# Wide blocks of a hybrid decoder trunk: all 512-column products of a block ahead of all its 256-column products

## The reference, cut to what matters

```python
    for i in range(DEPTH):
        h = rms_norm(x, norm1_g[i]) * (1.0 + sc1) + sh1
        if i % N_MIXERS == 0:
            mix = dilated_attention(h, attn_w_in[j], attn_w_out[j])
        else:
            mix = s5_mixer(h, ssm_w_in[j], ...)
        x = x + g1 * mix
        h = rms_norm(x, norm2_g[i]) * (1.0 + sc2) + sh2
        x = x + g2 * conv_ffn(h, ffn_w_up[i], ffn_conv_w[i], ffn_conv_b[i], ffn_w_down[i])
```

## Time and profile before

| | before |
|---|---|
| median of 3 runs | 2727.33 us (2723.91 to 2728.22) |
| span of the profiled execution | 2724.8 us |
| TensorE busy, matmuls | 2659.1 us (98%), 18416 |
| TensorE busy, weight loads | 2376.3 us (87%) |
| VectorE busy | 2299.6 us (84%) |
| ScalarE busy | 1294.9 us (48%) |
| GpSimd busy | 518.8 us (19%) |
| mean granted TensorE clock | 0.990 |

### The profile page before, as it was taken

The page is one execution under the profiler, slowest core; times in us unless marked ns, Lnnn a source line. Parts: engine busy times, 40 slices in busy tenths (PEclk is TensorE's granted clock), DMA queues, the critical chain, the costliest instruction groups (busy, mean ns, idle before and its releaser), DMA issues.

```text
span 2724.8 us, 50038 instructions
## 1 busy us (share of the span) xinstructions
PE 2659.1 (98%) x18416; PEld 2376.3 (87%) x18416; DVE 2299.6 (84%) x3379; ACT 1294.9 (48%) x1869; POOL 518.8 (19%) x468
## 2 busy tenths in 40 slices
PE   6999999999999999999999999999999999999998
PEld 2998888888898888888889998999888888888887
DVE  6978988888889998899999988998898975677754
ACT  2444444444434555435555344444365553455543
POOL 4242211101132111000111321244411110011122
PEclk8999999999999999999999999999999999999999
DMA  9989989889876987678888967779777766655563
GB/s 388 386 268 342 344 313 338 314 314 334 317 225 226 320 283 245 203 253 311 283 279 275 375 221 230 235 249 332 254 256 252 257 182 190 194 190 187 182 189 116
DMA packets 242267, 725.47 MB, mean 266 GB/s; under 512 B 51106, under 2 KB 60066, under 8 KB 241186
## 3 DMA queue, kind: packets, MB, share of 16 engines
q1 hardware_dynamic: 185184, 666.46, 71.1%
q10 hardware_dynamic: 56900, 56.54, 6.6%
HBM read 701.66 MB, written 25.44 MB: 267 GB/s over the span
## 4 chain that ended last, share of the span: by engine, by line
PE 84%; DVE 4%; POOL 1%; DMA 1%; issue 1%; ACT 1%; ACTq 0%; DVEq 0%; POOLq 0%
PE proj L1936 40%; PE proj L1939 22%; PE proj L1959 5%; PE proj L1960 5%; PE proj L1961 5%; PE proj L1941 3%; PE proj L1954 1%; DVE w_lo L1201 1%; PE proj L1957 1%; PE ps L2077 1%; PE ps L2167 1%; ACT w_hi L605 0%; DVE work L1484 0%; PE pturn L2194 0%; POOL work L1784 0%
## 5 line engine op out<-in xcount | busy, mean ns | idle before, releaser
L605 ACT ACTIVATE w_hi<-raw 128x1024 fp32r<-128x1024 f32 (+1 forms) x896 | 933.0, 1044 | 992.1 <-PE proj L1939 355.2
L1201 DVE TENSOR_TENSOR w_lo<-raw,w_hi 128x1024 fp32r<-128x1024 f32 (+1 forms) x896 | 1107.2, 1238 | 288.7 <-ACT w_hi L605 276.7
L1936 PE MATMUL proj<-h_hl,w_hi 128*128 128x512 f32 x3990 | 1007.5, 393 | 2.6 <-DVE x L1531 1.7
L1936 PEld LDWEIGHTS proj<-h_hl,w_hi 128*128 128x128 f32 x3990 | 730.5, 189 | 139.2 <-DVE x L1531 2.1
L1939 PEld LDWEIGHTS proj<-h_hl,w_lo 128*128 128x128 f32 x4256 | 580.6, 190 | 41.5
L1939 PE MATMUL proj<-h_hl,w_lo 128*128 128x256 f32 x4256 | 593.4, 282 | 0.0
L1091 DVE SCALAR_TENSOR_TENSOR ada<-ada,held 128x1024 f32<-128x1024 f32 x304 | 392.4, 1291 | 0.0
L1834 POOL TENSOR_TENSOR a_hl<-work,a_hl 128x256 fp32r<-128x256 f32 (+1 forms) x88 | 119.7, 1360 | 1137.3 <-ACT a_hl L895 1137.3
L1959 PE MATMUL proj<-a_hl,w_hi 128*128 128x256 f32 x864 | 245.6, 284 | 0.7 <-DVE a_hl L1422 0.6
L1960 PE MATMUL proj<-a_hl,w_hi 128*128 128x256 f32 x864 | 244.6, 283 | 0.0
L1961 PE MATMUL proj<-a_hl,w_lo 128*128 128x256 f32 x864 | 244.5, 283 | 0.0
(11 more groups left out here) (279 smaller groups left out, 2873.3 us busy)
## 6 DMA issues: line engine op xcount, KB each, us to landing
raw<-in_w_up SPq DMA_DIRECT2D x352, 512.0 KB, 4.9
ada<-in_ada_t SPq DMA_DIRECT2D x304, 512.0 KB, 5.7
raw<-in_w_in SPq DMA_DIRECT2D x224, 512.0 KB, 6.4
raw<-in_w_down SPq DMA_DIRECT2D x128, 448.0 KB, 3.7
raw<-in_w_down SPq DMA_DIRECT2D x64, 512.0 KB, 3.7
ada<-in_ada_w SPq DMA_DIRECT2D x48, 512.0 KB, 8.7
raw<-in_w_out SPq DMA_DIRECT2D x32, 512.0 KB, 4.7
raw<-in_ssm_w_in SPq DMA_DIRECT2D x32, 512.0 KB, 4.8
```

What stands on the lines that cost most here:

```text
L605: nc.scalar.activation(w_hi[:, j % LAG, 0:nk * P], raw[:, j % s.ring, 0:nk * P], ACT.Copy).then_inc(hi_ready, 1)
L1201: V.tensor_tensor(w_lo[:, j % LAG, 0:nk * P], raw[:, j % s.ring, 0:nk * P], w_hi[:, j % LAG, 0:nk * P].bitcast(F32), ALU.subtract).then_in ...
L1936: ins = mm(both, w_hi[:, j % LAG, w], hl[:, k].rearrange("p c t -> p (c t)"), start=(k == 0), stop=False)
```

## The change

`highs` issues the 512-column matmuls of a piece and waits for the high part alone (and, in a block's first piece, for the bank). `lows` issues its 256-column matmuls, waits for the low part, and signals `piece_done`. In a step of a wide block TensorE now does the `highs` of the step's piece, and in the step of the block's last piece it then does the `lows` of all pieces of the block in order. A stream's first block (its first two where pieces of two blocks are interleaved at the start) goes through `piece` as before, there too with `highs` and `lows` of the piece in a row.

```diff
+                def highs(i, j):
+                    b, k0, nk, last = s.pieces[j]
+                    if k0 == 0:
+                        wait(pe, block_out, s.block(i, b) - 1)
+                    pe.wait_ge(hi_ready, s.number(i, j) + 1)
+                    hl = a_hl if hi is a_hi else h_hl
+                    for k in range(k0, k0 + nk):
+                        mm(proj[b % 2][:, :], w_hi[:, j % LAG, (k - k0) * P:(k - k0 + 1) * P],
+                           hl[:, k].rearrange("p c t -> p (c t)"), start=(k == 0), stop=False)
+
+                def lows(i, j, signals):
+                    b, k0, nk, last = s.pieces[j]
+                    pe.wait_ge(lo_ready, s.number(i, j) + 1)
+                    for k in range(k0, k0 + nk):
+                        ins = mm(proj[b % 2][:, 0:T], w_lo[:, j % LAG, (k - k0) * P:(k - k0 + 1) * P], hi[:, k, :],
+                                 start=False, stop=(last and k == k0 + nk - 1))
+                    if signals:
+                        ins.then_inc(piece_done, signals)
...
+                    elif s.wide and not (isinstance(i, int) and i == 0 and s.pieces[j][0] < 1 + bool(cross)):
+                        highs(i, j)
+                        if s.pieces[j][3]:
+                            for m in range(j + 1 - sum(p[0] == s.pieces[j][0] for p in s.pieces), j + 1):
+                                lows(i, m, 1)
                     else:
                         piece(i, j, 1)
```

More of the change, by code:

```diff
@@ L1933, in piece @@
                     if s.wide and not first and not cut_at:
[L1934 to L1944, removed]
+                        highs(i, j)
+                        lows(i, j, signals)
                         return
```

## The result

| | before | change |
|---|---|---|
| median | 2726.21 us (20 runs, 2723.49 to 2728.55) | 2730.80 us (20 runs, 2727.03 to 2736.16) |
| ratio | | 1.0017, 95% interval 1.0011 to 1.0023 |
| span of the profiled execution | 2724.8 us | 2730.8 us |

The account below looks back on a forecast made before the run. TensorE, busy 98% of 2724.8 us, was taken as the bound, through matmul spacing and its waits. Terms -5.8 + 1.0 + 1.7 + 0.9 + 1.3 + 1.4 = +0.5 gave 2727.8 us, after 2.5 from span to median; range 2722 to 2737.

Parts of the forecast that it names:

- the likeliest case: Whole kernel: gain and losses cancel as summed, -5 to +5 us, chance 0.60.
- Waiting for the high part alone is worth nothing: Wide blocks: TensorE never waited for a low part there, so dropping that wait gains nothing by itself.
- Spacing, 6.4 us saved, 5.8 net: Wide blocks: 356 merges of matmul runs at 0.018 us each save 6.4 us, net 5.8.
- Down0a's share: Down0a: its 0.6 us of the merged-run saving is lost again at the bank wait of up0b.
- Steady rounds of qkv, 1.0 us: qkv after the first round: bank just fits or 0.1 late, transposes 0.1 late per head; 1.0 us lost, bounds 0 and 4.5.
- First round of qkv, 1.7: qkv's first round: bank 0.7 us late, two transposes later by about 0.5 each; 1.7 us lost, bounds 0.7 and 3.
- End of qkv, 0.9: End of qkv: the last gather comes later behind a low part and the scores wait for it; 0.9 us lost.
- ssm_out, 1.3: ssm_out: 1.0 us for the bank in the block with two row pieces, 0.3 for six with one; 1.3 lost.
- Norm, 1.4: Norm behind ssm_out: the last block's additions, for which the mean waits, come later; 1.4 us lost, not hidden.
- the slower one: qkv: bank and transpose both late in each of 10 heads, +6.5 us in sum, 2734 us; chance 0.23.

Follow-up runs that it names:

- hi_wait: Kernel before, same matmul order, but in wide blocks the 512-column matmuls wait for the high part alone: 2727.81 us, ratio 1.0003.
- Late_signal: Kernel before, only piece_done of all but a wide block's last piece moved onto the next piece's second 256-column matmul: 2737.44 us, ratio 1.0041.
- updown: The change in the up and down streams only, qkv and ssm_out in the order of before: 2722.48 us, 0.9984 of the kernel before.
- turned: Kernel before, but every second piece of a wide block does its 256-column matmuls first, merging runs with the first signal unmoved: 2721.11 us, ratio 0.9979.
- Split4: Kernel before, with each piece of up and down cut in two, the old order within each half: 2730.42 us, ratio 1.0015.
- one_block: The change, with pieces 6 and 7 of each qkv pass (one block in every second head) in the old order: 2727.59 us, 1.0005 of before.
- split_best: Kernel before, given the order of turned (in down, the change's order) and two signals per piece: 2726.75 us, ratio 1.0001.
- change_again: The changed kernel itself, unaltered, timed and profiled once more: 2729.88 us, 1.0014 of the kernel before.
- Old_where_late: The change, with qkv pieces 6, 7, 20 and 21 and the last block of ssm_out in the old order: 2722.59 us, 0.9990 of before.

## Why the prediction was nearly right, and where it was off

The median lay 3.0 us above the forecast, and the +4.6 only just inside the -5 to +5 of the likeliest case; the interval reaches past it. So the range held, but most of a loss had been put at nearly nothing.

- **Waiting for the high part alone is worth nothing:** shown by hi_wait.
- **Spacing, 6.4 us saved, 5.8 net:** shown. Late_signal and the change differ by 5.8 in the medians and by 6.2 in the stages; down1a got 0.59 shorter for 0.58; updown gave 4.5 for 3.9, turned 5.9 for 5.3. Down0a's share was lost again at the bank wait, as forecast: up0b took 248.1 us before and after. The even gap that I took from the Trainium skill (TensorE: Matmul & The Clock Gate, Back-to-back issue gap), which the page gives for an isolated matmul, gives no saving at all, and these runs rule that out. Split4 confirms that it is the start of a run that costs.
- **Steady rounds of qkv, 1.0 us: the step that failed, in size.** The bank was as worked out: read out until 537.25 in the head above, 0.17 ahead of the block, never late in any head. The transpose was not: 0.45 in each of 10 heads, 4.5 us, my upper bound. I had reasoned from one add, which would fall in VectorE's hole, and taken 0.1 per head. The Trainium skill (SBUF — State Buffer, SBUF: two separate sides) was right about that add. I didn't follow the chain to its end: the next low part then met a later add. The shift by rows alone gave the right number. The mechanism, the signal, is shown by late_signal (nothing moved but it) and by one_block (taken back in one block, gone in that head). That the adds are stretched beside VectorE is read from the durations, here and in split_best; no run isolates it.
- **First round of qkv, 1.7:** one bank wait of 0.77 (0.7 expected); the transposes of the two heads later by 0.6 and 0.45 in all, where I had 0.5 each; the first block with a transpose got 0.6 shorter and a bank wait behind it 0.3 longer, which I had not seen. The two heads took 89.6 us before and 91.1 after, 1.5 more with 0.2 saved by their merged runs in it: 1.7. That the sum met the forecast is partly luck, since two terms that I had not seen nearly cancel.
- **End of qkv, 0.9:** the wait for the scores rose from 0.34 to 1.2, so 0.9.
- **ssm_out, 1.3:** 1.0 as worked out for the block with two row pieces; nothing for the six others, where I had put 0.3.
- **Norm, 1.4:** 1.3 at the mean, as worked out; 1.9 by the next stream's first product, 1.5 in change_again. The part beyond the mean, the clock that falls earlier in a longer wait among it, I had put at nothing. Old_where_late takes all of it away.

With what was measured the sum is -5.8 + 4.5 + 1.7 + 0.9 + 1.0 + 1.9 = +4.2 us (3.8 with the norm of change_again), inside the interval of 3.0 to 6.3. The span's +6.0 holds more than the change: down0b's late transfer, and the time behind the last stream, which is 12.0 us in some profiles and 12.6 to 12.8 in others, in old and new orders alike. Of the rivals, the slower one named the right place with half of its mechanism: the transposes were late as it said, the bank was not.

## What to carry to other kernels

When a change delays a signal, follow every chain behind it to the last instruction that TensorE waits for, beside its neighbour engine all the way: an add that gets quicker in a new gap is no gain while the next one still falls beside the other engine's work. An order of matmuls and the release of their buffers are separate: here one and the same order costs 4.6 us with one signal for a piece and gains 7.8 with two, and an order that merges nearly as many runs without a later signal gains 5.9. And an earlier start is not always safe: turned runs with two signals (split_best) lost their whole gain, by the durations because VectorE then ran beside GpSimd.

## What I had not expected of the hardware

The 512-column matmuls keep their 0.227 us across the change of bank: in turned, a run of 16 that covers the end of one block and the start of the next has this spacing from the seventh on. The clock can fall in one execution of a kernel and not in another. Windows of PE at the start of up0b, where TensorE waits for the bank; the figure behind the last busy time is the granted clock. The change, first profile:

```profile
1246.00:1250.00 4.00, 2.21 (x11) 1.63 (x10) 3.86 (x12) 0.00 (x0) 0.00 (x0) 1.00 0.66 219
1250.00:1254.00 4.00, 4.00 (x26) 3.52 (x25) 3.93 (x11) 1.53 (x3) 0.00 (x0) 1.00 0.88 336
```

The same kernel, second profile:

```profile
1246.00:1250.00 4.00, 2.21 (x11) 1.59 (x10) 3.90 (x11) 0.19 (x1) 0.00 (x0) 0.96 0.72 241
1250.00:1254.00 4.00, 4.00 (x13) 3.15 (x12) 3.90 (x11) 1.33 (x2) 0.00 (x0) 0.61 0.87 343
```

After the same wait for the bank, 1.8 us, the clock was granted at 0.61 on average over four microseconds (between the levels of 1.2 and 2.4 GHz) and only 13 matmuls ran there instead of 26; up0b, without its last part, took 205.4 us against 203.5. Of these 1.9 us the clock explains 1.4, measured from the first matmul behind the wait to the end of the second block; 0.5 is a longer wait for a low part ahead of it (1.0 against 0.5). The same fall stands in the profile of one_block (0.59 over four microseconds). How often each kernel meets it is not known from one or two profiles. One such fall is worth 1.4 us, and one late transfer 2.0 (down0b above), so a change of this size is read from the stages and not from one span.
